# A fourth pair of rows as seven-product blocks in the gate/up projection, with the bank mixing moved one chunk later

## The reference, cut to what matters

```python
h = rms_norm(x, ffn_norm)
return x + (jax.nn.silu(h @ w_gate) * (h @ w_up)) @ w_down
```

## Time and profile before

| | |
|---|---|
| time of the kernel, median of 3 runs | 1110.89 us (1107.88 to 1111.1) |
| the profiled execution's own time | 1110.28 us |
| span in the profile | 1108.6 us |
| granted TensorE clock, mean | 0.997 |
| TensorE busy | 1094.4 us, 99% |
| VectorE busy | 833.1 us, 75% |
| ScalarE busy | 600.3 us, 54% |
| DMA queue q1 | 206.58 MB, 54.0% of 16 engines' span |

### The profile page before, as it was taken

One profiled execution on the slowest core, in us unless ns is written; L12 is line 12 of the kernel. 1 busy time (PEld: TensorE's weight loads), 2 busy tenths in 40 slices (PEclk: granted clock), 3 DMA queues, 4 the chain that ended last, 5 costly groups with the idle time before them and its releaser, 6 DMA issues.

```text
span 1108.6 us, 13405 instructions
## 1 busy us (share of the span) xinstructions
PE 1094.4 (99%) x5161; PEld 909.4 (82%) x5161; DVE 833.1 (75%) x760; ACT 600.3 (54%) x593; POOL 38.0 (3%) x44
## 2 busy tenths in 40 slices
PE   9999999999999999999999999999999999999997
PEld 6788889997888888888888888888888888788876
DVE  6444457664576798898898898898888878898793
ACT  6644346656655555454554555555554656475552
POOL 0380000000000000000000000000000000000000
PEclk9999999999999999999999999999999999999998
DMA  9765644653445555555555555556555655555551
GB/s 348 257 190 191 194 143 127 200 181 115 152 153 189 187 193 192 196 201 207 189 194 196 212 192 190 194 192 219 189 189 197 233 215 190 190 190 192 214 201 76
DMA packets 58323, 212.53 MB, mean 192 GB/s; under 512 B 4016, under 2 KB 11952, under 8 KB 41008
## 3 DMA queue, kind: packets, MB, share of 16 engines
q1 hardware_dynamic: 56288, 206.58, 54.0%
q10 hardware_dynamic: 2000, 5.46, 1.3%
HBM read 209.93 MB, written 2.10 MB: 191 GB/s over the span
## 4 chain that ended last, share of the span: by engine, by line
PE 93%; DVE 2%; DMA 2%; ACT 1%; issue 1%; SPq 0%; DVEq 0%; ACTq 0%
PE ps L1498 59%; PE ps L1274 9%; PE ps L1276 9%; PE ps L1275 9%; PE ps L1313 2%; DMA raw<-in_w_in 1%; DMA raw<-in_w_dn 1%; PE ps L1411 1%; PE ps L1361 1%; PE ps L1462 1%; PE ps L1464 1%; PE ps L1463 1%; PE ps L1360 0%; DVE mix L1227 0%; ACT w_hi L409 0%
## 5 line engine op out<-in xcount | busy, mean ns | idle before, releaser
L1498 PE MATMUL ps<-w_hi,xp_hi 128*128 128x512 f32 x539 | 211.7, 393 | 0.0
L1498 PE MATMUL ps<-w_hi,xp_lo 128*128 128x512 f32 x539 | 209.9, 389 | 0.0
L1498 PE MATMUL ps<-w_lo,xp_hi 128*128 128x512 f32 x539 | 209.7, 389 | 0.0
L816 DVE TENSOR_TENSOR w_lo<-raw,w_hi 128x2048 fp32r<-128x2048 f32 (+2 forms) x44 | 91.9, 2088 | 87.9 <-ACT w_hi L409 87.9
L1008 DVE TENSOR_TENSOR w_lo<-raw,w_hi 128x2048 fp32r<-128x2048 f32 x55 | 125.8, 2287 | 34.5 <-ACT w_hi L621 34.5
L621 ACT ACTIVATE w_hi<-raw 128x2048 fp32r<-128x2048 f32 x55 | 105.1, 1911 | 62.2 <-DMA raw<-in_w_gu 62.2
L1274 PE MATMUL ps<-w_hi,xT_hi 128*128 128x512 f32 (+1 forms) x352 | 132.7, 377 | 1.2 <-DVE w_lo L816 1.2
L1276 PE MATMUL ps<-w_hi,xT_lo 128*128 128x512 f32 (+1 forms) x352 | 131.0, 372 | 0.0
L1275 PE MATMUL ps<-w_lo,xT_hi 128*128 128x512 f32 (+1 forms) x352 | 130.9, 372 | 0.0
L710 ACT ACTIVATE w_hi<-raw 128x2048 fp32r<-128x2048 f32 (+1 forms) x44 | 80.1, 1821 | 85.2 <-DMA raw<-in_w_dn 85.1
L1498 PE MATMUL ps<-w_hi,xo_hi 128*128 128x512 f32 x302 | 118.5, 392 | 3.6 <-DVE ps L1132 3.6
(11 more groups left out here) (235 smaller groups left out, 1867.1 us busy)
## 6 DMA issues: line engine op xcount, KB each, us to landing
raw<-in_w_gu SPq DMA_DIRECT2D x88, 1024.0 KB, 4.8
raw<-in_w_dn SPq DMA_DIRECT2D x44, 1024.0 KB, 4.8
raw<-in_w_in SPq DMA_DIRECT2D x34, 1024.0 KB, 5.1
raw<-in_w_out SPq DMA_DIRECT2D x16, 1024.0 KB, 5.1
raw<-in_w_in SPq DMA_DIRECT2D x8, 576.0 KB, 3.8
raw<-in_w_ukv SPq DMA_DIRECT2D x3, 1024.0 KB, 5.1
raw<-in_w_uq SPq DMA_DIRECT2D x3, 768.0 KB, 4.4
xT_raw<-in_xT SPq DMA_DIRECT2D x4, 512.0 KB, 8.3
```

The lines of the kernel that those rows point to most:

```text
L816: nc.vector.tensor_tensor(w_lo[n % 4][:, 0:k, 0:c], raw[n % 4][:, 0:k, 0:c], w_hi[n % 4][:, 0:k, 0:c].bitcast(F32), ALU.subtract).then_inc ...
L1498: mm = nc.tensor.matmul(out, x, wt, start=start and j + m == 0, stop=stop and 3 * j + m == n - 1, skip_group_check=resumed)
```

## The change

`SUMS` becomes (0, 2, 4, 5), so c5 is a seven-product chunk as well, and the last one of a strip. The mixing moves behind it: `mix_sums` and half 0 go to step 5, `part_done` to the middle of c6, half 1 to the end of c6, and the waits for `mixed` to c7. On VectorE half 1 is now put between the additions ("s") and the subtractions ("l") of the preparation of c8. In the last strip it stands behind the whole of `down_lo(0)`. c6 and c7 both do banks 0 and 1 first, so the ScalarE and VectorE waits for `ffn_done` change with them. The preparation of c5 waits until TensorE has finished c2, because both use the second `t_sum` buffer. The token sums of pair 5 are made one chunk later than its transposes were (steps 63 and 64), and `H0` and `sf` move to make room for the larger `xp` buffers.

```diff
-SUMS = (0, 2, 4)
+SUMS = (0, 2, 4, 5)
-for _step, _pairs in ((58, (0, 1)), (59, (2, 3)), (62, (4, 5)), (FF0, (6, 7))):
+for _step, _pairs in ((58, (0, 1)), (59, (2, 3)), (62, (4,)), (63, (5,)), (FF0, (6, 7))):
-XS_SPLIT = {59: 0, 60: 1, 63: 2}
+XS_SPLIT = {59: 0, 60: 1, 63: 2, 64: 3}
-        H0 = 153 * K
+        H0 = 156 * K
-        sf = at("sf", H0 + 64 * K, [4, P])
+        sf = at("sf", 144 * K, [4, P])
...
-                    if p == 4:
+                    if p == SUMS[-1]:
                         act.wait_ge(mix_done, i * 2 + 1)
...
-                            act.wait_ge(ffn_done, i * 3 + (2 * b + 1))
+                            act.wait_ge(ffn_done, i * 3 + (b + 1))
...
                 if "s" in parts:
                     dve.wait_ge(raw_in[slot], i * (4 * FB) + 16 * (n // 4 + 1))
+                    if p == SUMS[-1]:
+                        dve.wait_ge(chunk_used, i * FB + (FF0 + SUMS[1] + 1))
...
-                    if p == 4:
+                    if p == SUMS[-1]:
                         mix_sums(i)
                         mix_banks(i, 0, None)
-                    if p == 5:
-                        mix_banks(i, 1, i * FB + (FF0 + 6))
...
-                                dve.wait_ge(ffn_done, i * 3 + 2)
+                                dve.wait_ge(ffn_done, i * 3 + 3)
...
                     if last and p + AHEAD >= FB:
                         down_lo(p + AHEAD - FB)
+                        if p == SUMS[-1]:
+                            mix_banks(i, 1, i * FB + (FF0 + 7))
+                    elif p == SUMS[-1]:
+                        prep_lo(i, p + AHEAD, "s")
+                        mix_banks(i, 1, i * FB + (FF0 + 7))
+                        prep_lo(i, p + AHEAD, "l")
                     else:
                         prep_lo(i, p + AHEAD)
...
-                sides = ((0, 0), (1, 0), (0, 1), (1, 1)) if p in (5, 6) else ((0, 0), (0, 1), (1, 0), (1, 1))
+                sides = ((0, 0), (1, 0), (0, 1), (1, 1)) if p > SUMS[-1] else ((0, 0), (0, 1), (1, 0), (1, 1))
...
-                    if p == 6 and g % 2 == 0:
+                    if p == SUMS[-1] + 2 and g % 2 == 0:
                         pe_.wait_ge(mixed, i * 2 + (g // 2 + 1))
...
-                    if p == 5 and g == 1:
+                    if p == SUMS[-1] + 1 and g == 1:
                         mm.then_inc(part_done, 1)
```

More of the change, by code:

```diff
@@ L196, in build @@
         junk_f = at("junk_f", H0 + 52 * K, [TOK, COLS])
-        SM = H0 + 66 * K
+        SM = H0 + 64 * K
         ident = at("ident", SM, [P])
@@ L1525, in sums_chunk @@
                     if first and not late:
-                        after(unit_act, "a", ("xt2", 5))
-                        after(unit_dve, "v", ("xt2", 5))
+                        after(unit_act, "a", ("xs2", 5))
+                        after(unit_dve, "v", ("xt2", 3))
                     elif not first:
@@ L1572, in plain_chunk @@
                                [xp_lo[p][:, j, toks] for j in range(2)], [w_hi[slot][:, j, :] for j in cols],
-                               [w_lo[slot][:, j, :] for j in cols], p == 1 and g == 3, p in (5, FB - 1), resumed=p > 5)
-                    if p == 5 and g == 1:
+                               [w_lo[slot][:, j, :] for j in cols], p == 1 and g == 3, p > SUMS[-1], resumed=p == SUMS[-1] + 2)
+                    if p == SUMS[-1] + 1 and g == 1:
                         mm.then_inc(part_done, 1)
```

## The result

The changed kernel takes 1140.86 us (median of 4 runs, 1138.96 to 1142.56), the kernel before 1110.97 us (4 runs). The ratio is 1.0273, 95% interval 1.0252 to 1.0294: slower by 30 us. The forecast was 1128.5 us with a range of 1117 to 1136: the direction was right, the size too small. The profiled execution took 1142.56 us, with a span of 1140.8 us.

The account below looks back on a forecast made before the run. TensorE sets the pace now; after the change VectorE was to be slowest, with waits through the mixing. First strip 6.8, strips 9.8, last strip 0.2, clock 1.4: 18.2 us on 1110.28 gives 1128.5 us, range 1117 to 1136.

Parts of the forecast that it names:

- The reserve: VectorE's idle time beside TensorE in a strip of the kernel before: 4.5 us, against 4.67 us of added work.
- What the change takes from TensorE: c5 goes from 24 to 21 matmuls: 0.68 us less a strip, 7.5 us in all.
- The strips: Looped strips go from 42.50 to 43.48 us through VectorE's work and new waits: +9.8 us over ten steps.
- the one at c11: VectorE's start of c11, 7.45 us after c10's in place of 6.87, because ScalarE is late; c11 starts at 19.73.
- The ring that I named: Half 0, VectorE's preparations up to c13, TensorE's c13 and half of c14, the next half 0: 43.48 us.
- My sign for strips over 44.5 us: Strips this long in the new profile would show the prediction wrong at the clock.
- The first strip: Half 0 of the first strip comes later, 430.4 instead of 423.63: +6.8 us, 4.76 from the mixing's later place.
- The last strip and the clock: Half 1 behind `down_lo(0)` stops TensorE for 5.8 us: +0.2 us, and +1.4 us for a clock fall behind it.
- B: Rival: the cover holds and TensorE keeps the pace, 1108.6 or 1105.6 us; chance 0.04 faster, 0.05 within 0.3%.
- A: Rival: VectorE is full but the loop through the mixing doesn't close; strips 42.7 us, time 1120.7; chance 0.17.
- C: Rival: the clock also falls in the strips at the wait ahead of c13, 14 us in all, 1142.5; chance 0.18.
- D: Rival: the mixing holds c7 in every strip, cover 0.3 us, costless until 0.9 us late; within the forecast's range.

Follow-up runs that it names:

- m1: The kernel before, with only the mixing moved one chunk later and c5 left a plain chunk: 1146.45 us (ratio 1.0329).
- d2: The kernel before, with VectorE's first weight addition of c4 made twice over in addition (2.5 us more a strip): 1115.1 us (ratio 1.0048).
- d4: The kernel before, with VectorE's first weight addition of c4 made four times over in addition (5.0 us more a strip): 1153.86 us (ratio 1.0395).
- e1: The changed kernel, with ScalarE's first copy of the hidden tile put ahead of t_hi of c10: 1126.56 us (ratio 1.0148).
- x2: The changed kernel, with VectorE making t_lo of c5 for two of four blocks only (1.07 us less): 1140.2 us (ratio 1.0273).
- e4: The changed kernel, with the last strip's half 1 right behind the first down chunk's three weight additions: 1137.59 us (ratio 1.0248).
- w0: The changed kernel, with hidden copy ahead of c10's t_hi, c8's additions ahead of half 0, last strip's half 1 earlier: 1117.85 us (ratio 1.0074).

## Why the prediction was wrong, point by point

**What bounds the kernel.** TensorE at 0.227 us a matmul with the strip at 42.50 us was read rightly. The reserve was read as VectorE's 4.5 us of idle time. That isn't where the reserve was: ring A stood at 42.5 us already, and m1, with no more VectorE work than before, lost 2.84 us a strip. d2 and d4 show the same on another ring, the one through c4: its reserve was 2.4 us, not 4.5.

**What the change takes from TensorE.** 0.68 us a strip: m1 against the changed kernel gives 45.34 - 44.65 = 0.69 us.

**The strips: +9.8 us predicted, +21.5 us measured.** Ten strips took 446.5 us (431.10 to 877.63) against 425.0 before. The step that failed is the one at c11: "the two copies of the hidden tile come 1.83 and 0.49 us later". I had read the 0.49 us as the distance of two copies on ScalarE (they lie 1.43 us apart in the earlier trace rows), and left out that between them lie transposes on TensorE that wait for the first copy and, in turn, delay every chunk behind them. In the earlier trace rows the second copy is marked as waiting for TensorE. Who waits for the first copy, I didn't ask; in the kernel before it shows only as the 0.3 us of the weight loads. With it, the prediction's own clock (12.28 us up to c10's additions instead of 14.86, and 4.76 us more on TensorE) gives 42.50 - 2.58 + 4.76 = 44.68 us. The ring that I named (half 0 to c13 and back) is real, and e1 shows it at 43.2 us once ring A is cut. In the changed kernel it didn't decide: c13 was ready at 646.39 (644.10 + 2.29) and TensorE came for it at 646.69, so TensorE's predicted wait ahead of c5 doesn't appear, and x2 brings nothing. My sign for strips over 44.5 us pointed at the clock, which was wrong as well: it was granted in full (1.00).

**The first strip: +6.8 us predicted, +7.5 us measured** (431.10 against 423.63; 0.8 us of it lay already ahead of the altered steps, where VectorE's last low part before them came at 379.81 instead of 378.97).

**The last strip and the clock: +1.6 us predicted, +3.2 us measured.** Half 1 came 9.80 us behind half 0 (887.43 - 877.63), just as predicted, and TensorE stood still for 5.67 us (5.8). The clock's fall was under-sized: the 12 matmuls of the second half of c7 took 5.28 us (888.71 to 893.99) instead of 2.72, so 2.6 us, where I had taken 1.4. That a fall would come after a wait of that length was right. One of the two rows had it so, and so did the Trainium skill, "TensorE: Matmul & The Clock Gate", section "Why this matters for your kernels".

**The added wait for c2, half 1's cover, the silu waits:** none of them cost anything, as forecast; VectorE has no wait for c2 in the trace.

**The rivals.** B (faster or same) was wrong. A's value of 42.7 us a strip came true only with two reorderings, and even there VectorE wasn't full. C put its price on the clock in the strips; in the changed kernel the clock stayed at 1.00 there, and the time of 1142 us that C gave was met by another cause. In d4, with waits of 2.5 us, its mechanism does show. D did not decide in the changed kernel, where TensorE has no wait for a mixed bank in the looped strips. No rival had the hidden tile.

## What to carry to other kernels

When work moves in a software pipeline, the idle time of an engine says little. Write down, for each wait that crosses engines, the closed ring on which it lies, with one period's work on it, and compare each ring with the period; the tightest ring here had no slack while its engines showed 5 and 20 us of idle time. A step moved later by one chunk puts that chunk into the ring from this step to the next time it comes; here that was 4.76 us, less the 2.61 us that moved out of the ring. And where an engine has several small jobs to do, put first the one that the bounding engine waits for: one copy moved ahead of a larger one was worth 14 us of 1141.

## What the runs showed of the hardware

GpSimd's 128x512 float32 subtraction, 1.6 us at best and up to 3.4 us beside VectorE, slowed VectorE's subtractions by more than it relieved them (5.61 us for two of 1.75 us each).

A wait of TensorE of 2.5 us that recurs at the same place of each strip was followed by a fall of the granted clock every other time, so two neighbouring strips with the same work lasted 45.32 and 46.95 us. Behind the single wait of 5.67 us the clock was at its lower level (0.50 of full) for the whole of the following 5 us. Behind a wait of 2.99 us at the same place of two kernels, e4 and w0, it fell in e4 and stayed at 1.00 in w0. Waits of 0.83 and 1.55 us, one of each in a strip of the changed kernel, were followed by no fall at all.
